# Picking two experts' token rows straight into turned form, from the fp32 x, with two more load buffers

## The reference

```python
x = x + jnp.matmul(merged, w_out)                  # the attention part, ends with "x after"
x = x + hier_moe(rms_norm(x, g_ffn), w_grp, b_grp, w_rt, b_rt, w_gate, w_up, w_down)
gate = jax.nn.sigmoid(jnp.matmul(rms_norm(x, g_ple), w_ple_gate))
x = x + gate * jnp.matmul(p_i, w_ple_proj)
...
def block_fn(args):                                # one block of rows of one expert e_b
    tok_b, e_b = args
    xb = h_pad[tok_b]                              # rows of the tokens that chose the expert
    hid = jax.nn.silu(jnp.matmul(xb, w_gate[e_b])) * jnp.matmul(xb, w_up[e_b])
    return jnp.matmul(hid, w_down[e_b])
```

## Time and profile before

| What | Value |
|---|---|
| median of 3 runs | 999.1 us (998.84 to 1000.87) |
| profiled execution, device time | 998.48 us |
| its span, first to last instruction | 996.7 us |
| mean granted TensorE clock | 0.997 |
| PE busy | 967.7 us, 97% of the span |
| DVE / ACT / POOL busy | 380.4 / 305.9 / 134.7 us |
| moved by DMA | 256.05 MB, mean 257 GB/s |
| chain that ended last | PE 81%, DMA 12%, DVE 2%, POOL 2%, ACT 2% |

### The profile page before, as it was taken

How to read it: one execution, slowest core, us unless ns; L and a number is a source line. 1 busy time by engine, 2 the same in 40 slices (tenths; PEclk the granted TensorE clock), 3 DMA queues, 4 the chain that set the end, 5 groups by cost and what they waited for, 6 DMA issues and landing times.

```text
span 996.7 us, 12099 instructions
## 1 busy us (share of the span) xinstructions
PE 967.7 (97%) x4818; PEld 593.6 (60%) x4818; DVE 380.4 (38%) x785; ACT 305.9 (31%) x536; POOL 134.7 (14%) x137
## 2 busy tenths in 40 slices
PE   8999999999999999999999999999998998999996
PEld 6776887676788888886434444444443443443475
DVE  4344896655353536327211111110111111013776
ACT  6445335746433214242111111111111111211555
POOL 0320234926500000000000100000000000001000
PEclk9999999999999999999999999999999999999998
DMA  9512230000082350856999999999999999999902
GB/s 333 183 49 79 85 92 2 2 1 2 1 296 85 94 195 7 350 201 249 414 391 423 419 421 421 422 421 420 421 420 420 421 420 422 415 421 405 369 1 85
DMA packets 59145, 256.05 MB, mean 257 GB/s; under 512 B 12222, under 2 KB 12862, under 8 KB 34000
## 3 DMA queue, kind: packets, MB, share of 16 engines
q1 hardware_dynamic: 50224, 248.26, 62.4%
q0 software_dynamic: 2560, 4.20, 1.1%
q10 hardware_dynamic: 6304, 2.80, 1.1%
HBM read 248.95 MB, written 10.49 MB: 260 GB/s over the span
## 4 chain that ended last, share of the span: by engine, by line
PE 81%; DMA 12%; DVE 2%; POOL 2%; ACT 2%; issue 0%; DVEq 0%; SPq 0%
PE psum L749 37%; PE psum L1119 17%; DMA slot<-in_w_up 12%; PE psum L1075 5%; PE psum L1139 4%; PE psum L1140 4%; PE psum L1095 1%; PE psum L1159 1%; PE psum L1261 1%; PE psum L1085 1%; PE psum L964 1%; PE psum L949 1%; PE psum L937 1%; POOL raw L2211 1%; PE psum L737 1%; PE psum L925 1%
## 5 line engine op out<-in xcount | busy, mean ns | idle before, releaser
L1119 PE MATMUL psum<-slot,xt 128*64 128x512 f32 x512 | 232.7, 598 | 10.1 <-DMA slot<-in_w_up 9.4
L1120 PE MATMUL psum<-slot,xt 128*64 128x512 f32 x512 | 232.9, 598 | 0.0
L1119 PEld LDWEIGHTS psum<-slot,xt 128*64 128x64 f32 x512 | 65.8, 137 | 131.9 <-issue 127.7
L1139 PE MATMUL psum<-slot,ht 128*64 128x512 f32 x256 | 115.9, 595 | 0.0
L1140 PE MATMUL psum<-slot,ht 128*64 128x512 f32 x256 | 115.9, 596 | 0.0
L749 PE MATMUL psum<-w_hi,act_hi 128*128 128x512 f32 x288 | 114.8, 399 | 0.3 <-DVE act_lo L1655 0.3
L2227 POOL DMA_INDIRECT pair_rows<-y,slot_pair x30 | 30.3, 1012 | 618.3 <-ACT y L1500 618.3
L749 PE MATMUL psum<-w_lo,act_hi 128*128 128x512 f32 x288 | 112.5, 391 | 0.0
L749 PE MATMUL psum<-w_hi,act_lo 128*128 128x512 f32 x288 | 112.3, 390 | 0.0
L574 DVE TENSOR_TENSOR w_lo<-raw,w_hi 128x2048 fp32r<-128x2048 f32 (+1 forms) x30 | 69.3, 2308 | 90.3 <-ACT w_hi L569 90.2
L1493 ACT ACTIVATE small<-psum,slot_inv 64x512 f32<-64x512 f32 x32 | 21.9, 684 | 250.3 <-PE psum L1120 249.3
(11 more groups left out here) (294 smaller groups left out, 1490.1 us busy)
## 6 DMA issues: line engine op xcount, KB each, us to landing
slot<-in_w_gate SPq DMA_DIRECT2D x64, 1024.0 KB, 21.2
slot<-in_w_up SPq DMA_DIRECT2D x64, 1024.0 KB, 20.7
slot<-in_w_down SPq DMA_DIRECT2D x64, 1024.0 KB, 22.0
raw<-in_w_in SPq DMA_DIRECT2D x21, 1024.0 KB, 5.1
raw<-in_w_out SPq DMA_DIRECT2D x4, 1024.0 KB, 5.7
pair_in<-pair_rows SPq DMA_DIRECT2D x4, 1024.0 KB, 14.8
slot<-in_w_ple_gate SPq DMA_DIRECT2D x4, 1024.0 KB, 12.3
rows_tok<-in_x SPq DMA_DIRECT2D x8, 256.0 KB, 5.2
```

Of the source, the lines that this page charges most:

```text
L1119: mm_g = pe.matmul(ps[FIRST:2 * FIRST, :], left, g[:, k, :], start=first, stop=last)
L1120: mm_u = pe.matmul(ps[0:FIRST, :], left, u[:, k, :], start=first, stop=last)
L1139: pe.matmul(ps[0:FIRST, :], left, w[:, k, 0:512], start=first, stop=last)
```

## The change

Rows are picked and turned in one step. `gather(q, g)` multiplies x itself in fp32: the stationary operand is a slice of `xres`, 128 tokens by 128 columns taken at a step of 8 elements, and the moving operand is `pick` (now fp32, 128 places). For each of 8 slices, 4 tiles of tokens are added up in one part of a bank. The first half (g = 0) stands between `gate_up(e+1)` and `down(e)`, the second behind `down(e)`, where the transposes stood. `x1_hi`, `x1_lo`, their casts and subtractions, the additions that bring x back, `copy_rows` and `turn_x` go. `x1t` becomes a ring of four tiles of half the size. The memory of `stage` becomes two more slots (19), and the loads into `stage` and `rope` now come first and wait for the branch product and the gates instead. ACT's wait for `slots_set` now stands ahead of one small DMA issue. The projection waits for `xt_done`.

```diff
-SLOTS = 17
+SLOTS = 19
...
-SLOT_REGION = [("qk", 0), ("qk", 1), ("more", 0)] + [("raw", (N_FRONT - RAW + k) % RAW) for k in range(RAW)]
+SLOT_REGION = [("stage", 0), ("stage", 1), ("rope", 0), ("qk", 0), ("qk", 1), ("more", 0)]
+RAW_FROM = len(SLOT_REGION)
+SLOT_REGION += [("raw", (N_FRONT - RAW + k) % RAW) for k in range(RAW)]
...
-        while last and SLOT_REGION[k][0] in ("v", "rope", "more"):
+        while last and SLOT_REGION[k][0] in ("v", "rope", "more", "stage"):
...
-    x1t = sb("x1t", "v", [P, KD, S])[:]
-    x1_hi = sb("x1_hi", "stage", [P, NT, D], F32R)[:]
-    x1_lo = sb("x1_lo", "o", [P, NT, D], F32R)[:]
-    pick = sb("pick", "lo", [P, NT, 2 * FIRST], F32R, skip=14 * K)[:]
+    x1t = sb("x1t", "v", [P, 4, 4, P])[:]
+    pick = sb("pick", "lo", [P, NT, 2 * FIRST], skip=14 * K)[:]
...
+            elif SLOT_REGION[n][0] == "stage":
+                filled(sp, ("branch_b", 1, "tile", NT - 1))
+            elif SLOT_REGION[n][0] == "rope":
+                drained(sp, ("gate_b", 1, "tile", NT - 1))
...
-        def gather(q, between=None):
-
-            if q == 0:
-                pe.wait_ge(x1_hi_done, NT)
+        def gather(q, g):
+
+            if q == 0 and g == 0:
+                for t in range(NT):
+                    drained(pe, ("out", 1, "tile", t))
                 pe.wait_ge(first_picked, 1)
-            else:
+            if q:
                 pe.wait_ge(picked, q + 1)
-                pe.wait_ge(x_copied, 2 * q)
-                pe.wait_ge(xt_done, 2 * q)
+                pe.wait_ge(xt_done, 2 * q + g - 1)
...
-            for h in range(2):
-                for part in (x1_hi, x1_lo):
-                    for t in range(NT):
...
-                        mm = pe.matmul(bank[(1, 7)[h]], pick[:, t, :], by_chunk(part[:, t], h),
-                                       start=part is x1_hi and t == 0, stop=part is x1_lo and t == NT - 1)
-                    if between and h and part is x1_hi:
-                        between()
-                mm.then_inc(x_gathered, 1)
-
-        def turn_x(q, g):
-
-            pe.wait_ge(x_copied, 2 * q + g + 1)
             for k in range(4):
-                mm = pe.transpose(bank[g][:, k * P:(k + 1) * P], x_rows[:, 512 * g + k:512 * (g + 1):4], ident)
+                for t in range(NT):
+                    if (q, g, k, t) == (0, 0, 0, NT // 2):
+                        pe.wait_ge(picked, 1)
+                    mm = pe.matmul(bank[g][:, k * P:(k + 1) * P], xres[:, t, 4 * g + k:D:KD], pick[:, t, :], start=t == 0,
+                                   stop=t == NT - 1)
             mm.then_inc(x_turned, 1)
...
-        gather(0, lambda: turn_x(0, 0))
+        for g in range(2):
+            gather(0, g)
...
             if e % 2 and e + 3 < NE:
-                gather(e // 2 + 2)
+                gather(e // 2 + 2, 0)
             pe.wait_ge(ht_done, e + 1)
             down(e, (lambda: turn_and_wait(NE - 1)) if e == NE - 2 else None)
...
             if e % 2 and e + 3 < NE:
-                for g in range(2):
-                    turn_x(e // 2 + 2, g)
+                gather(e // 2 + 2, 1)
...
-        def copy_rows(q):
-            if q:
-                act.wait_ge(x_turned, 2 * q)
-            for h in range(2):
-                act.wait_ge(x_gathered, 2 * q + h + 1)
-                act.copy(x_rows[:, h * 512:(h + 1) * 512], bank[(1, 7)[h]]).then_inc(x_copied, 1)
-
-        copy_rows(0)
+        act.wait_ge(slots_set, 3)
         act.dma_start(g_tail[:], g_ple[0].rearrange("(k p) -> p k", p=P), allow_slow_non_contiguous=True).then_inc(g_tail_in, 16)
-        act.wait_ge(slots_set, 3)
         silu(0)
...
             if q:
-                dve.wait_ge(x_gathered, 2 * q)
+                dve.wait_ge(x_turned, 2 * q)
```

More of the change, by code:

```diff
@@ L242 @@
 EXPERT_HALVES = expert_halves()
-SLOT_REGION = [("qk", 0), ("qk", 1), ("more", 0)] + [("raw", (N_FRONT - RAW + k) % RAW) for k in range(RAW)]
+SLOT_REGION = [("stage", 0), ("stage", 1), ("rope", 0), ("qk", 0), ("qk", 1), ("more", 0)]
+RAW_FROM = len(SLOT_REGION)
+SLOT_REGION += [("raw", (N_FRONT - RAW + k) % RAW) for k in range(RAW)]
 SLOT_REGION += [(r, n % SPLIT) for n in range(N_FRONT - SPLIT, N_FRONT - 1) for r in ("whi", "wlo")]
-SLOT_REGION += [("hi", 0), ("lo", 0)] + [(r, (N_FRONT - 1) % SPLIT) for r in ("whi", "wlo")] + [("v", 0), ("rope", 0)]
+SLOT_REGION += [("hi", 0), ("lo", 0)] + [(r, (N_FRONT - 1) % SPLIT) for r in ("whi", "wlo")] + [("v", 0)]
 assert len(SLOT_REGION) == SLOTS
@@ L394, in layer_kernel @@
     no_rows = sb("no_rows", "small", [P, D // 2], skip=4 * K)[:]
-    last_pick = [sb("last_pick_0", "lo", [P, NT, 2 * FIRST], skip=14 * K)[:], sb("last_pick_1", "stage", [P, NT, 2 * FIRST])[:]]
+    last_pick = [sb(f"last_pick_{n}", "lo", [P, NT, 2 * FIRST], skip=(14, 10)[n] * K)[:] for n in range(2)]
     to_token = sb("to_token", "gain", [P, 2, S], F32R)[:]
@@ L474, in layer_kernel @@
     p_turned, pt_copied, proj_filled = sem("p_turned"), sem("pt_copied"), sem("proj_filled")
-    x1_hi_done, x1_low, first_picked, x1_back, tail_added = (sem(n) for n in (
-        "x1_hi_done", "x1_low", "first_picked", "x1_back", "tail_added"))
-    picked, x_gathered, x_copied, halves_made = sem("picked"), sem("x_gathered"), sem("x_copied"), sem("halves_made")
+    first_picked, tail_added, picked, halves_made = (sem(n) for n in ("first_picked", "tail_added", "picked", "halves_made"))
     (tail_turned, tail_high, tail_ready, tail_filled, tail_gated, tail_squared, tail_rms, tail_inv, added, last_squared,
@@ L678, in load_slot @@
             elif SLOT_REGION[n][0] == "raw":
-                sp.wait_ge(lo_done, N_FRONT - RAW + n - 3 + 1)
-            elif SLOT_REGION[n][0] in ("whi", "wlo") and n < 3 + RAW + 2 * (SPLIT - 1):
-                sp.wait_ge(half_started, N_FRONT - SPLIT + 2 + (n - 3 - RAW) // 2)
+                sp.wait_ge(lo_done, N_FRONT - RAW + n - RAW_FROM + 1)
+            elif SLOT_REGION[n][0] in ("whi", "wlo") and n < RAW_FROM + RAW + 2 * (SPLIT - 1):
+                sp.wait_ge(half_started, N_FRONT - SPLIT + 2 + (n - RAW_FROM - RAW) // 2)
             elif SLOT_REGION[n][0] in ("hi", "lo"):
                 sp.wait_ge(half_started, N_FRONT)
-            elif SLOT_REGION[n][0] in ("v", "rope"):
+            elif SLOT_REGION[n][0] == "v":
                 sp.wait_ge(logits_done, 1)
@@ L820, in route_x1 @@
             for k in range(4 * h, 4 * h + 4):
-                mm = pe.matmul(bank[0][:, t * w:(t + 1) * w], x1t[:, k, t * P:(t + 1) * P], wr[:, k, :], start=False,
+                mm = pe.matmul(bank[0][:, t * w:(t + 1) * w], x1t[:, j % 4, k % 4, :], wr[:, k, :], start=False,
                                stop=(k, t) == (KD - 1, NT - 1))
@@ L1051, in count_members @@
                 pe.matmul(bank[7][0:1, 0:1], c("ones")[:, 0:1], over_f[:, 0:1], start=True, stop=True).then_inc(list_done, 1)
-        def gather(q, between=None):
-            if q == 0:
-                pe.wait_ge(x1_hi_done, NT)
+        def gather(q, g):
+            if q == 0 and g == 0:
+                for t in range(NT):
+                    drained(pe, ("out", 1, "tile", t))
                 pe.wait_ge(first_picked, 1)
-            else:
+            if q:
                 pe.wait_ge(picked, q + 1)
-                pe.wait_ge(x_copied, 2 * q)
-                pe.wait_ge(xt_done, 2 * q)
+                pe.wait_ge(xt_done, 2 * q + g - 1)
             if q == PROJ_E // 2 + 2:
                 pe.wait_ge(proj_done, 2 * NT)
[L1064 to L1067, removed]
-            for h in range(2):
-                for part in (x1_hi, x1_lo):
-                    for t in range(NT):
[L1071 to L1074, removed]
-                        mm = pe.matmul(bank[(1, 7)[h]], pick[:, t, :], by_chunk(part[:, t], h),
-                                       start=part is x1_hi and t == 0, stop=part is x1_lo and t == NT - 1)
-                    if between and h and part is x1_hi:
-                        between()
-                mm.then_inc(x_gathered, 1)
-        def turn_x(q, g):
-            pe.wait_ge(x_copied, 2 * q + g + 1)
-            for k in range(4):
-                mm = pe.transpose(bank[g][:, k * P:(k + 1) * P], x_rows[:, 512 * g + k:512 * (g + 1):4], ident)
+            for k in range(4):
+                for t in range(NT):
[3 more added lines that the diff above has]
+                                   stop=t == NT - 1)
             mm.then_inc(x_turned, 1)
@@ L1147, in project @@
             loaded(0, "p", 0)
+            pe.wait_ge(xt_done, PROJ_E + 4)
             for i in range(PLE // P):
@@ L1171, in _ @@
             if e == 0:
-                gather(1)
+                gather(1, 0)
             if e % 2 and e + 3 < NE:
-                gather(e // 2 + 2)
+                gather(e // 2 + 2, 0)
             pe.wait_ge(ht_done, e + 1)
@@ L1177, in _ @@
             if e == 0:
-                for g in range(2):
-                    turn_x(1, g)
+                gather(1, 1)
             if e % 2 and e + 3 < NE:
```

(20 more changed lines are left out.)

10 lines of the change are left out of this document (removed).

## The result

The changed kernel takes 1156.7 us (median of 4 runs, 1156.3 to 1157.4) against 999.1 us: a ratio of 1.1575, 95% interval 1.1557 to 1.1593. It is slower by 157.7 us, where 38 were forecast. The span of the profiled execution is 1155.6 us, and 94% of its chain is PE.

A forecast was written before the change was run, and what follows sets the result against it. PE was taken to bound the kernel, with weight transfers close behind. Terms 41.7 + 2.6 + 2.8 + 0.3 - 9.4 gave +38.0 us, a forecast of 1037 us, range 1027 to 1073 us.

The forecast's parts named there:

- The bound: Expert stage: PE would bound each round, 30.6 us against 29.9 us of transfers, so added PE work costs its full length.
- waits for weights: PE's waits for expert weights, between about 713 and 834 us, would go as rounds lengthen: -9.4 us.
- The count: New gather on PE: 32 fp32 matmuls of two instructions, so 64 per pair of experts, about 1024 in all.
- the line 1024 p - 85: Whole run: change in us against the old kernel, with p the time of one PE instruction of the gather.
- The step: Gather's stationary loads of x at 8 elements: taken as 0.12 us each, making a pair's preparation 8.08 us, 2.98 more.
- The upper bound: Gather's load at a step of 8: at most 0.180 us, from 0.111 plus the 69 ns a transpose's load gains.
- Rival C: Gather on PE: loads hide, columns set the pace, 0.053 us per instruction; supply bounds, 994 us; chance 0.05.
- Rival D: Expert rounds: forecast PE cost plus new waits, 15 x 0.5 us, +8, 1045 us; chance 0.70 together with the main forecast.
- the late SiLU: ACT's table load comes behind the scales, so SiLU starts some 1.7 us later; 1.4 covered, +0.3 us.
- q = 0: First pair's preparation on PE: 8.08 us in place of 5.08, less 0.15 from an earlier start, +2.8 us.
- The first loads: Three expert loads start before 390 us rather than at 400.77, filling memory earlier: 0 us.
- The tail: End of the run: the planner keeps 14 slots from expert 24 on in both kernels, so length unchanged, 0 us.

The follow-up runs named there:

- experiment 5: The changed kernel with 17 slots for loads in place of 19: 1156.8 us, against 1156.7 with 19.
- experiment 2: The changed kernel with the gather's stationary slices of x at a step of 4 elements, then 2, in place of 8: 1151.0 us and 1033.7 us.
- experiment 8: The changed kernel with 17 slots and the gather in fp32r on x rounded once, step 8, low part left out, 512 loads: 1065.1 us.

## Why the prediction was wrong

The direction, the bound and the count held; one term was mis-sized, and it is the one called the unknown.

- **The bound** was right. PE bounds every round, its waits for weights are gone (-9.4 us), and slots bring nothing there (experiment 5).
- **The count** was right: 1024 instructions, all on the path. At the measured pace of 0.237 the line 1024 p - 85 gives +158 us; the result is +157.7. So the other terms hold in sum. The round grew by 10.5 us; 64 x 0.237 + 0.4 - 5.1 is 10.5.
- **The step** is the term that failed. I took 0.12 us for a load at a step of 8, with an upper bound of 0.180; it is 0.237. 1024 x (0.237 - 0.12) = 120 us, which is the whole gap between +38 and +157.7. The row was a transpose's, and its price was carried over in two ways, as a floor and as 69 ns on top. Neither holds for a load that reads in another way: an ordinary load at the very same step of 4 paces at 0.233 where the transpose's paces at 0.119 (experiment 2).
- **The upper bound.** With hindsight a wider one could be worked out of the same rows. Loads overlap, and about 80 ns of each are not paced by its columns (the 64-column loads of both kernels last 137 ns, the 128-column ones 190, so 53 ns per 64). Taken off a transpose's 141 and 210 ns, 60 becomes 130, a factor of 2.2; times the 0.111 us of the contiguous pace that is 0.24. That it hits the measured value may be luck, for it fails on the transposes themselves: at a step of 8 their 195 ns make 115 of 60, and their pace stays at 0.111. But a range with this factor in it would have reached to 1160 us.
- **Rival C** (a cheap narrow product) fell, by 0.112 us even without a step. The 81 ns that the Trainium skill gives there (TensorE: Matmul & The Clock Gate, section Back-to-back issue gap) do not hold for these fp32 instructions: 0.112 us at a step of 1.
- **Rival D** (new waits) did not come: PE's waits in the stage sum up to 1.4 us, 0.2 of them for the late SiLU, where I had 0.3.
- **q = 0** took 15.4 us from 456.58 us on, all of it the new p; its start came 0.6 us earlier than in the earlier trace rows, more than the 0.15 I gave.
- **The first loads** leave at 395.99 us, not ahead of 390; since nothing waits for them it costs nothing.
- **The tail** is 67.6 us, as before.

## What to carry to other kernels

Choose which operand is stationary by counting loads and by how it lies in memory, not by columns alone: a product of 128 columns or fewer with a new stationary operand each time ran at the pace of the loads here, and in fp32 it needs two of them. Where an ordinary stationary operand is read at a step of 16 bytes or more (16 to 64 were measured), count each load double; lay it out once with another engine, or leave the turning to transposes, whose pace stayed between 0.111 and 0.119 us at steps of 16 and 32 bytes. When a price has to be taken from another kind of instruction, it is a guess: bound it by the factor between the two rows as well as by their difference, and measure that term first if most of the sum hangs on it.

## What the runs showed of the hardware

- The pace of an ordinary 128x128 fp32 load by the step of its columns, in us: 0.112 at 1, 0.118 at 2, 0.233 at 4, 0.237 at 8, 0.239 at 9 ((7.74 - 0.34) / 31), 0.218 at 16 ((7.06 - 0.31) / 31). fp32r loads last as long as fp32 ones at a step of 8 (336 and 334 ns).
- A transpose's load lasts 141 ns contiguous and 210 at a step of 4, but on average 195 with most of them at 8; its pace is 0.103, 0.119 and 0.111 us. Why transposes are spared was not settled.
- The pace is that of the loads and not of the columns that move: eight contiguous loads with products of one column come at (0.99 - 0.19) / 7 = 0.114 us in the changed kernel, as with 128 columns:

```profile
573.10 0.99 PEld L1038 LDWEIGHTS psum<-cst,small 128*128 128x128 f32 x8
```

- ACT may have the same kind of price: a copy of 1024 columns read at a step of 8 lasts 2.05 to 2.22 us, the cast of the same tile read in order 1.04 us. The one is a copy and the other a cast, so the step alone is not shown to make the difference.
- TensorE's granted clock can fall to the lower level behind a block in which PE mostly waits for its own loads, although the profile shows PE busy all through. It did so in 18 places of the fp32r kernel (experiment 8). With the two-instruction fp32 products at the same pace of loads it seldom did: the changed kernel has one such stretch in its expert stage, behind the block at 565.5 us and the eight one-column products at 573.1 us (granted clock 0.53 over 3.6 us), and the kernels with steps of 4, 9 and 16 have none. What sets the two apart was not settled:

```profile
574.20:577.80 3.60, 3.60 (x10) 1.08 (x12) 0.66 (x2) 0.00 (x0) 0.00 (x0) 0.53 0.02 5
```
